# Second MLP's up products: one 512-column product for both activation parts, and a copy and an add for its second half

## What is computed

```python
def _conv_glu_ffn(h, w_up, conv_w, conv_b, w_down):
    u = _causal_depthwise_conv(h @ w_up, conv_w, conv_b)   # w_up: 1024 x 5632
    gate, val = jnp.split(u, 2, axis=-1)                   # 2816 channels each
    return (jax.nn.silu(gate) * val) @ w_down              # w_down: 2816 x 1024

for l in range(DEPTH):                                     # DEPTH = 2
    ...                                                    # attention half of the layer
    h = _rms_norm(x, norm2_gain[l]) * (1.0 + sc2) + sh2
    x = x + g2 * _conv_glu_ffn(h, w_ffn_up[l], ffn_conv_w[l], ffn_conv_b[l], w_ffn_down[l])
return _rms_norm(x, final_gain)
```

## Time and profile before

| | |
|---|---|
| median of 3 runs | 723.14 us (723.10 to 723.15) |
| profiled execution, its own time | 724.23 us |
| its span, first to last instruction | 722.4 us |
| mean granted TensorE clock | 0.991 of full |
| second MLP, first up product to last down product | 524.42 to 713.35 us |

### The profile page before, as it was taken

How to read it: one execution, slowest core, us unless ns; L and a number is a source line. 1 busy time by engine, 2 the same in 40 slices (tenths; PEclk the granted TensorE clock), 3 DMA queues, 4 the chain that set the end, 5 groups by cost and what they waited for, 6 DMA issues and landing times.

```text
span 722.4 us, 15359 instructions
## 1 busy us (share of the span) xinstructions
PE 698.9 (97%) x6436; PEld 659.9 (91%) x6436; DVE 501.1 (69%) x901; ACT 397.3 (55%) x639; POOL 122.4 (17%) x96
## 2 busy tenths in 40 slices
PE   7899999999999999999999999989999999999995
PEld 6798988899999999999999998869999999999993
DVE  1454888647888879797666478863687666666666
ACT  2258646834746465656446674663574555544552
POOL 2001003004054635453010000300400000000002
PEclk9999999999999999999999999999999999999998
DMA  9999987465485857588753874646526577555511
GB/s 329 392 275 287 391 282 280 176 233 176 131 316 196 292 176 293 175 291 284 279 162 116 303 271 150 229 180 235 175 88 210 137 244 248 184 175 175 182 52 58
DMA packets 97739, 159.43 MB, mean 221 GB/s; under 512 B 6119, under 2 KB 84744, under 8 KB 91400
## 3 DMA queue, kind: packets, MB, share of 16 engines
q1 hardware_dynamic: 97672, 158.46, 64.0%
HBM read 156.81 MB, written 1.64 MB: 219 GB/s over the span
## 4 chain that ended last, share of the span: by engine, by line
PE 78%; DVE 9%; ACT 5%; issue 3%; SPq 2%; DMA 1%; POOL 0%; DVEq 0%; POOLq 0%; ACTq 0%
PE bank L965 23%; PE bank L966 22%; PE bank L967 22%; PE bank L978 3%; DVE w_lo L1650 2%; ACT work L1535 2%; DVE score L1831 1%; DMA own_bias<-in_buckets 1%; PE bank L1258 1%; ACT w_hi L1396 1%; DVE top L1830 1%; PE bank L1011 1%; SPq L711 1%; SPq L731 1%; PE bank L1289 1%
## 5 line engine op out<-in xcount | busy, mean ns | idle before, releaser
L1650 DVE TENSOR_TENSOR w_lo<-raw,w_hi 128x2048 fp32r<-128x2048 f32 (+1 forms) x97 | 237.0, 2443 | 96.6 <-ACT w_hi L1396 96.4
L965 PE MATMUL bank<-act_hi,w_hi 128*128 128x256 f32 (+1 forms) x1024 | 292.9, 286 | 0.8 <-DVE act_lo L1667 0.7
L966 PE MATMUL bank<-act_lo,w_hi 128*128 128x256 f32 (+1 forms) x1024 | 289.6, 283 | 0.0
L967 PE MATMUL bank<-act_hi,w_lo 128*128 128x256 f32 (+1 forms) x1024 | 289.6, 283 | 0.0
L1396 ACT ACTIVATE w_hi<-raw 128x2048 fp32r<-128x2048 f32 (+1 forms) x97 | 183.0, 1888 | 143.8 <-PE bank L967 133.3
L965 PEld LDWEIGHTS bank<-act_hi,w_hi 128*128 128x128 f32 (+1 forms) x1024 | 195.5, 191 | 4.5 <-issue 3.4
L966 PEld LDWEIGHTS bank<-act_lo,w_hi 128*128 128x128 f32 (+1 forms) x1024 | 195.6, 191 | 0.4
L967 PEld LDWEIGHTS bank<-act_hi,w_lo 128*128 128x128 f32 (+1 forms) x1024 | 195.5, 191 | 0.0
L1952 DVE SCALAR_TENSOR_TENSOR work<-bank,vec,work 128x254 f32<-128x254 f32 (+1 forms) x176 | 76.5, 476 | 11.1 <-ACT work L1594 9.6
L965 PE MATMUL bank<-mlp_hi,w_hi 128*128 128x256 f32 x192 | 54.7, 285 | 0.0
L966 PE MATMUL bank<-mlp_lo,w_hi 128*128 128x256 f32 x192 | 54.3, 283 | 0.0
(11 more groups left out here) (205 smaller groups left out, 942.8 us busy)
## 6 DMA issues: line engine op xcount, KB each, us to landing
direct<-in_w_ada SPq DMA_DIRECT2D x48, 1024.0 KB, 8.6
raw<-in_w_ffn_up SPq DMA_DIRECT2D x44, 1024.0 KB, 5.2
raw<-in_w_ffn_down SPq DMA_DIRECT2D x22, 1024.0 KB, 4.9
raw<-in_w_in SPq DMA_DIRECT2D x21, 1024.0 KB, 6.5
raw<-in_w_out SPq DMA_DIRECT2D x8, 1024.0 KB, 5.0
bias<-toeplitz SPq DMA_DIRECT2D x4, 384.0 KB, 11.6
xT<-in_x SPq DMA_DIRECT2D x1, 1024.0 KB, 5.1
raw<-in_w_in SPq DMA_DIRECT2D x2, 512.0 KB, 11.0
```

The costliest lines, as they stand in the source:

```text
L965: pe.matmul(dst, lh, rh, start=first, stop=False, skip_group_check=check)
L966: pe.matmul(dst, lh, rl, start=False, stop=False, skip_group_check=check)
L967: return pe.matmul(dst, ll, rh, start=False, stop=last, skip_group_check=check)
L1650: nc.vector.tensor_tensor(w_lo[n % RAW][:, s], raw[n % RAW][:, s], w_hi[n % RAW][:, s].bitcast(F32), ALU.subtract).then_inc(lo_done, 1)
```

## The change

Only the MLP of the second layer is touched, and of it steps 0 to 9; step 10 runs as before but for one more wait. `act_hi` and `act_lo` become views of one tile, `act_both`, in which the two parts of a k-tile lie side by side as 512 columns. For each k-tile and each tile of 128 channels, PE now multiplies `w_hi` by all 512 columns into a whole bank, and then `w_lo` by `act_hi` into that bank's first 256 columns. The bank's second half is then the product of `w_hi` with `act_lo`, which has to be added: ScalarE copies it to SBUF (`copy_rest`, into `tile_sum`, a piece of the attention's `qkT`), and VectorE adds the first half to it (`sum_tiles`). Taps read `tile_sum` and no longer the bank. A tile takes a bank of its own: in step 0 banks 0, 1, 2 and 4, in step 1 banks 0, 1, 2 and 7, after that banks 0, 1 and 2 in turn (`tile_bank`), so that tile 4j + 2*which + f waits for the sum of the tile three before it. Both `take_mod` of the MLP are done in step 0.

```diff
         w_lo = [sb(f"w_lo{i}", [P, KT * UC], F32R) for i in range(RAW)]
         direct = [sb(f"direct{i}", [P, KT * UC]) for i in range(DSLOTS)]
         xT = sb("xT", [P, KT, SEQ])
-        act_hi = sb("act_hi", [P, KT, SEQ], F32R)
-        act_lo = sb("act_lo", [P, KT, SEQ], F32R)
+        act_both = sb("act_both", [P, KT, 2, SEQ], F32R)
+        act_hi, act_lo = act_both[:, :, 0, :], act_both[:, :, 1, :]
         mlp_hi = sb("mlp_hi", [P, 2, SEQ], F32R)
         mlp_lo = sb("mlp_lo", [P, 2, SEQ], F32R)
         qkT = sb("qkT", [P, 4, 2, 2, SEQ])
...
         v_flat = v_sb[:, :, :, :].rearrange("p g t n -> p (g t n)")
         gate_row, gain_row = v_flat[:, 0:D_MODEL], v_flat[:, D_MODEL:2 * D_MODEL]
+        tile_sum = qkT[:, 0, :, :, :]
         gained = qkT[:, 2, :, :, :].rearrange("p a b t -> p (a b t)")
         squared = [qkT[:, g, half, :, :].rearrange("p b t -> p (b t)") for g in (1, 3) for half in range(2)]
...
         turn_hi = sem("turn_hi")
         turn_lo = sem("turn_lo")
         conv_read = sem("conv_read")
+        first_tile = sem("first_tile")
+        rest_copied = sem("rest_copied")
+        tile_summed = sem("tile_summed")
         silu_ready = sem("silu_ready")
         prod_done = sem("prod_done")
         mlp_hi_ready = sem("mlp_hi_ready")
...
         def out_part_of(ct):
             return bank[4][:, 0:SEQ] if ct == KT - 1 else bank[ct // 2][:, (ct % 2) * SEQ:(ct % 2 + 1) * SEQ]
+        def tile_bank(j, which, f):
+            return bank[(0, 1, 2, 7 if j else 4)[2 * which + f] if j < 2 else (4 * j + 2 * which + f - 8) % 3]
+        def both_parts(l, j):
+            return l + 1 == DEPTH and j < STEPS - 1
         def early_tiles(n):
...
                                                   heads_out[:, TURNS[i], t, w * P:(w + 1) * P], ident[:, :])
                         mm.then_inc(t_ready, 1)
+                def wide_tile(j, which, f, k0, k1, wait_act=None):
+                    n = unit_no(l, NI + NO + (which if j == 0 else 3 * j - 1 + which))
+                    pe.wait_ge(lo_done, n + 1)
+                    if j:
+                        tile = 4 * j + 2 * which + f
+                        pe.wait_ge(tile_summed, min(tile, 6) - 3 if tile < 8 else tile - (3 if tile < 11 else 2))
+                    wh = w_hi[n % RAW][:, :].rearrange("p (k n) -> p k n", k=KT)
+                    wl = w_lo[n % RAW][:, :].rearrange("p (k n) -> p k n", k=KT)
+                    s, dst = slice(f * P, (f + 1) * P), tile_bank(j, which, f)
+                    for k in range(k0, k1):
+                        if wait_act is not None:
+                            pe.wait_ge(act_lo_ready, wait_act + k + 1)
+                        pe.matmul(dst[:, :], wh[:, k, s], act_both[:, k, :, :].rearrange("p a t -> p (a t)"),
+                                  start=k == 0, stop=False, skip_group_check=True)
+                        mm = pe.matmul(dst[:, 0:SEQ], wl[:, k, s], act_hi[:, k, :], start=False, stop=k == KT - 1,
+                                       skip_group_check=True)
+                    if k1 == KT:
+                        mm.then_inc(unit_used if f else first_tile, 1)
+                def wide_first():
+                    for k in range(KT // 2):
+                        for which in range(2):
+                            for f in range(2):
+                                wide_tile(0, which, f, k, k + 1, None if which or f else KT * (norm + 1))
+                    for which in range(2):
+                        wide_tile(0, which, 0, KT // 2, KT, None if which else KT * (norm + 1))
+                        wide_tile(0, which, 1, KT // 2, KT)
+                def wide_up(j, which):
+                    for f in range(2):
+                        wide_tile(j, which, f, 0, KT)
                 def up_first():
                     for which, k0, k1 in [(which, k, k + 1) for k in range(KT // 2) for which in range(2)] + [
...
                         if k1 == KT:
                             mm.then_inc(unit_used, 1)
-                def up(j, which):
+                def single_up(j, which):
+                    if last:
+                        pe.wait_ge(tile_summed, 4 * j - 1 + which)
                     pe.wait_ge(conv_read, 2 * (STEPS * l + j - 1) + which + 1)
                     unit_product(l, NI + NO + 3 * j - 1 + which, bank[which]).then_inc(unit_used, 1)
...
                         mm = pe.transpose(bank[7][:, k * P:(k + 1) * P], xT[:, 4 * q + k, t * P:(t + 1) * P], ident[:, :])
                     mm.then_inc(rows_turned, 1)
-                down = down_rows if l + 1 == DEPTH else down_product
-                up_first()
+                last = l + 1 == DEPTH
+                down = down_rows if last else down_product
+                if last:
+                    wide_first()
+                else:
+                    up_first()
                 for j in range(1, STEPS):
+                    up = wide_up if both_parts(l, j) else single_up
                     up(j, 0)
                     if j == 1:
                         turned[0] = ada_no(*GAP_PAIRS[norm + 1][1]) + 2
                     elif l + 1 == DEPTH and j < 6:
+                        if j == 2:
+                            pe.wait_ge(tile_summed, 8)
                         turn_x(j - 2)
                     up(j, 1)
                     down(j - 1)
...
                 def last_tap(j, which):
                     o = which if j == 0 else 3 * j - 1 + which
-                    act.wait_ge(unit_used, first + o + 1)
+                    if both_parts(l, j):
+                        act.wait_ge(tile_summed, 4 * j + 2 * which + 2)
+                    else:
+                        act.wait_ge(unit_used, first + o + 1)
                     if j > 0:
                         act.wait_ge(prod_done, STEPS * l + j)
                     for f in range(2):
                         ch = which * FT + 2 * j + f
-                        nc.scalar.activation(conv[:, which, f, :], bank[which][:, f * SEQ:(f + 1) * SEQ], ACT.Identity,
+                        src = tile_sum[:, which, f, :] if both_parts(l, j) else bank[which][:, f * SEQ:(f + 1) * SEQ]
+                        nc.scalar.activation(conv[:, which, f, :], src, ACT.Identity,
                                              scale=vec[:, l, V_W2 + ch:V_W2 + ch + 1],
                                              bias=vec[:, l, V_CB + ch:V_CB + ch + 1]).then_inc(tap_ready, 1)
+                def copy_rest(j, which):
+                    for f in range(2):
+                        if f:
+                            act.wait_ge(unit_used, first + (which if j == 0 else 3 * j - 1 + which) + 1)
+                        else:
+                            act.wait_ge(first_tile, 2 * j + which + 1)
+                        nc.scalar.activation(tile_sum[:, which, f, :], tile_bank(j, which, f)[:, SEQ:2 * SEQ],
+                                             ACT.Copy).then_inc(rest_copied, 1)
                 for j in range(STEPS):
+                    if j and both_parts(l, j):
+                        copy_rest(j, 0)
                     if j < STEPS - 1:
                         split_hi(first + 3 * j + 2)
+                    if j == 0 and both_parts(l, j):
+                        copy_rest(j, 0)
                     last_tap(j, 0)
+                    if both_parts(l, j):
+                        copy_rest(j, 1)
                     split_hi(first + (3 * j + 3 if j < STEPS - 1 else 3 * STEPS - 1))
                     last_tap(j, 1)
                     act.wait_ge(conv_read, 2 * (STEPS * l + j) + 1)
...
                         for f in range(2):
                             ch = which * FT + 2 * j + f
                             dst = conv[:, which, f, lag:SEQ]
+                            src = tile_sum[:, which, f, :] if both_parts(l, j) else bank[which][:, f * SEQ:(f + 1) * SEQ]
                             ins = nc.vector.scalar_tensor_tensor(
-                                dst, bank[which][:, f * SEQ:(f + 1) * SEQ - lag], vec[:, l, tap + ch:tap + ch + 1], dst,
+                                dst, src[:, 0:SEQ - lag], vec[:, l, tap + ch:tap + ch + 1], dst,
                                 ALU.mult, ALU.add)
                             if lag == 1:
                                 ins.then_inc(dve_own, 1)
...
                             dve.wait_ge(dve_own, count[0])
                     ins.then_inc(conv_read, 1)
+                def sum_tiles(j, which):
+                    for f in range(2):
+                        dve.wait_ge(rest_copied, 4 * j + 2 * which + f + 1)
+                        into = tile_sum[:, which, f, :]
+                        nc.vector.tensor_tensor(into, tile_bank(j, which, f)[:, 0:SEQ], into, ALU.add).then_inc(
+                            tile_summed, 1)
                 for j in range(STEPS):
+                    if j and both_parts(l, j):
+                        sum_tiles(j, 0)
                     if j < STEPS - 1:
```

(9 more changed lines are left out.)

## The result

The changed kernel took 721.26 us (median of 20 runs, 719.20 to 723.45), the kernel before 725.44 us in the runs beside them (20 runs, 723.02 to 727.67). The ratio is 0.9948, with a 95% interval of 0.9935 to 0.9961: 2.8 to 4.7 us less. In a second set, on another occasion, the changed kernel took 721.56 us (12 runs) beside 723.74 (29 runs), a ratio of 0.9963 (0.9949 to 0.9978). The kernel became faster, as forecast; the time lies above the forecast's range, which ended at 720.8.

A forecast was written before the change was run, and what follows sets the result against it. PE's instruction stream was taken to bound the second MLP; 4.27 us from merged pairs plus 0.21 from the hole, 4.48 in all, took 724.23 to 719.75 us, carried to the median 718.7. The range was 718.2 to 720.8.

The forecast's parts named there:

- The bound: Second MLP: PE's own instruction stream sets the end, through how far apart products start.
- The 320 pairs, 4.27 us: Up products, steps 0 to 9: merging 320 pairs of narrow products into wide ones saves 0.0133 us each.
- Rival 2: Up products: alternating widths shed no per-product cost, a k-tile stays near 0.36 us; 722.9 us in all, chance 0.10.
- its halfway point: Up products: the outcome halfway into the case that alternating widths save little, put at 720.8 us.
- The estimate that I drew from the Trainium skill: Up products: by the page's issue gap a merged pair saves about 2.5 ns, the 320 pairs 0.8 us.
- The hole, 0.21 us: PE's wait before unit 1, for taps to read bank 0, goes: 0.33 us between products becomes 0.12.
- ScalarE and VectorE: Second MLP: 40 new copies at 0.40 us and 40 adds at 0.43 cost nothing as long as PE never waits.
- The last tap: ScalarE, second MLP: the last tap now reads SBUF, nearest row 0.506 us.
- The tightest place: Start of the second MLP: VectorE's split of step 1's value weights ends 0.4 us before PE wants them.
- Rivals 1 and 3: 1: VectorE or ScalarE late at start, 719.0 to 719.9 us, chance 0.14; 3: VectorE bounds steps 1 to 9, 729.8, 0.04.
- rival 3's point of decision: Steps 1 to 9: VectorE becomes the bound when an add of 1.3 us takes its step past PE's 16.5 us.
- Carried to the median: Whole kernel: the profiled 719.75 us, lowered by 1.09 us to the median of three runs, gives 718.7.

The follow-up runs named there:

- e1: Changed kernel with all wide products of a wide_tile call before its narrow ones: second MLP 184.88 us against 186.38; ratio to the kernel before 0.9946.
- e9: Changed kernel with narrow before wide in every second k-tile, giving runs of two: second MLP 184.55 us against 186.38; ratio to the kernel before 0.9949.
- e6: Changed kernel with products grouped by two k-tiles, two wide then two narrow: second MLP 184.73 us against 186.38, executed once.
- e7: Changed kernel with each add of sum_tiles done twice, first into unread SBUF: second MLP 187.09 us against 186.38, executed once.

## Why the prediction was right or wrong

*The bound.* Right. The second MLP is PE's own stream, and everything that made it shorter came from how far apart products start.

*The 320 pairs, 4.27 us.* The step that failed. The count was right and the sign, but a pair saved 0.0067 us and not 0.0133: 2.13 us. The failure is in "I take 4.27, as a wide product beside a load of 128x128 stands in the trace 264 times": I read the price in the middle of a run of 24 wide products and wrote that "the nearest difference is that the wide and the narrow now alternate", without looking for a row where a wide product follows narrow ones. The trace of before had it, at the start of each down product:

```profile
565.15 0.28 PE L967 MATMUL bank<-act_hi,w_lo 128*128 128x256 f32 x1
565.27 0.40 PE L965 MATMUL bank<-w_hi,mlp_hi 128*128 128x512 f32 x1
565.50 0.40 PE L966 MATMUL bank<-w_lo,mlp_hi 128*128 128x512 f32 x1
565.74 0.39 PE L967 MATMUL bank<-w_hi,mlp_lo 128*128 128x512 f32 x1
...
566.66 0.39 PE L965 MATMUL bank<-w_hi,mlp_hi 128*128 128x512 f32 x1
```

The first two take 0.47 us, 0.235 each, and the first six 1.39 us, 0.2317 each; only then 0.2267 begins. With 0.235 the term would have been 320 x 0.005 = 1.6 us, near the 2.13 measured. Rival 2, "what a product costs besides its columns isn't shed when wide and narrow alternate", was half right, and its halfway point, 720.8, is what 723.14 less 2.32 gives.

*What the alternation costs.* That the order of widths decides it is shown (e1, e9). Why is open. A pair took 0.3533 us in runs of one, 0.3481 in runs of two, 0.3494 in runs of four and 0.3488 in runs of eight, by the rows above; over the floor of 0.3467 that is 6.7, 1.4, 2.7 and 2.1 ns. Averaged over all such products of the stretch, by their starts in the trace, it is 6.6, 2.0, 3.8 and 2.6 ns, in the same order. Neither a fixed price per change nor one for lone products gives that series.

These averages show where the price lies. In runs of eight (e1) the first five wide products behind narrow ones start 230 to 235 ns apart and the rest 227 to 228, 28 ns too much in all eight, while the first narrow one behind wide ones takes 114 ns and not 120, 7 ns back in all: 21 ns net for eight pairs. In runs of two (e6) the two wide ones cost 13 ns too much and the two narrow ones give 9 back: 4 ns net for two pairs. The dearer products and the cheaper ones thus both stand just behind a change of width, and the net price depends on how many of each kind a run holds.

The estimate that I drew from the Trainium skill ("TensorE: Matmul & The Clock Gate", section "Back-to-back issue gap"), 2.5 ns saved per pair, was too low here: the trace shows 6.7 as the change was written, and 11.9 in runs of two.

*The hole, 0.21 us.* Right: 0.11 us between the two products where 0.33 were.

*ScalarE and VectorE.* Right that they cost nothing. Groups by form in the changed kernel (busy us, mean ns): the add was put at 0.43 us and the copy at 0.40.

```profile
L1654 ACT ACTIVATE work<-qkT,vec 128x256 f32<-128x256 f32 x40 | 21.7, 594 | 3.2 <-DVE qkT L2044 3.2
L2044 DVE TENSOR_TENSOR qkT<-bank,qkT 128x256 f32<-128x256 f32 x40 | 15.4, 417 | 10.0 <-ACT qkT L1665 9.9
L1665 ACT ACTIVATE qkT<-bank 128x256 f32<-128x256 f32 x40 | 14.6, 380 | 27.0 <-PE bank L1340 27.0
```

The last tap was not: from SBUF it took 0.594 us, more than the 0.552 from PSUM, where I had taken 0.506 from another form of instruction. The tightest place was where I put it. VectorE's split of the value weights

```profile
539.48 2.28 DVE L1726 TENSOR_TENSOR w_lo<-raw,w_hi 128x2048 fp32r<-128x2048 f32 x1
```

ended at 541.76, and PE took up the value unit 16 pairs after 536.66, at 542.31: 0.5 us to spare where I had 0.4, and e7 measures the same. Rivals 1 and 3 did not occur; e7 shows that with adds of twice the cost the start loses 0.7 us and the later steps next to nothing, which fits rival 3's point of decision (1.3 us an add).

*The time itself.* "Carried to the median" was a second weak step. 723.14 was the median of three runs within 0.05 us of each other; in the later sets the kernel before had medians of 723.7 to 725.4, since its front moves. The gain would have placed the changed kernel at 720.8, the end of the range. The rest of the way to 721.26, 0.4 us, lies in the front by the subtraction above: a start at 523.8 us, against 523.3 for the three runs.

## What to carry to other kernels

A price per instruction read in a run of equal instructions holds in such a run: before it is used for a new order, look for the rows where one kind follows the other, for example where two stages meet. Where a product is made wider to save what each product costs besides its columns, keep products of one width together, two at least, and try the length, since four did less well here than two or eight: turning the order in every second k-tile (e9) took another 1.8 us out of the stage, 4.15 us against before. And where one stage repeats to 0.04 us while whole runs differ by 4, measure the change in that stage.

## What the runs showed of the hardware

Products of 512 columns start 0.2267 us apart behind others of 512, some 0.235 behind products of 256, and those of 256 take 0.11 to 0.12 behind products of 512, all at the full granted clock and with weight loads of 0.19 us beside them. An ACTIVATE of 128x256 with a scale and a bias per row took 0.594 us from SBUF and 0.552 us from PSUM. One transfer of 1 MB of weights early in the kernel took 15.0 to 18.3 us from issue to landing in the 12 profiles.
